# One order of VectorE's work in a local attention, and one layer of compressed blocks with its operands exchanged

## The reference, cut to what matters

```
def compress_blocks(kv, pe, w1, w2):
    B, G, S, dh = kv.shape
    ncmp = (S - CMP_LEN) // CMP_STRIDE + 1
    idx = (jnp.arange(ncmp) * CMP_STRIDE)[:, None] + jnp.arange(CMP_LEN)[None, :]
    blk = kv[:, :, idx] + pe
    flat = blk.reshape(B, G, ncmp, CMP_LEN * dh)
    return jax.nn.gelu(flat @ w1, approximate=False) @ w2
```

## Time and profile before

| | |
|---|---|
| median of 3 runs | 4155.18 us (4150.83 to 4158.11) |
| the profiled execution, its time | 4158.37 us |
| its span | 4157.0 us |
| busy: PE / DVE / ACT / POOL | 3893.0 / 2502.8 / 1586.3 / 870.8 us |
| mean granted clock of TensorE | 0.961 |
| local attention, first scores to output projection | 2564.84 to 2684.40 us |
| first `blocks` to first merge gate tile | 3708.92 to 3746.26 us |

### The profile page before, as it was taken

One profiled execution on the slowest core, in us unless ns is written; L12 is line 12 of the kernel. 1 busy time (PEld: TensorE's weight loads), 2 busy tenths in 40 slices (PEclk: granted clock), 3 DMA queues, 4 the chain that ended last, 5 costly groups with the idle time before them and its releaser, 6 DMA issues.

```text
span 4157.0 us, 58493 instructions
## 1 busy us (share of the span) xinstructions
PE 3893.0 (94%) x23644; PEld 3421.5 (82%) x23644; DVE 2502.8 (60%) x5047; ACT 1586.3 (38%) x2380; POOL 870.8 (21%) x404
## 2 busy tenths in 40 slices
PE   7998998899999999999999998898999999888799
PEld 4667888778888888778888876698999999888699
DVE  4554555379606884057766655585772677756575
ACT  2323444333234553221111124444565333347453
POOL 0002333034543333400000000068666000000000
PEclk9998999899999999999999998899999999988899
DMA  5231000123444556556767742056778678632254
GB/s 180 96 118 35 1 1 1 31 85 130 146 144 168 180 200 235 167 187 231 262 225 247 244 137 67 26 159 203 230 238 268 228 270 279 228 112 82 87 163 157
DMA packets 225500, 649.38 MB, mean 156 GB/s; under 512 B 20048, under 2 KB 89552, under 8 KB 217424
## 3 DMA queue, kind: packets, MB, share of 16 engines
q1 hardware_dynamic: 119296, 401.92, 30.5%
q10 hardware_dynamic: 105936, 243.73, 16.3%
HBM read 543.33 MB, written 101.71 MB: 155 GB/s over the span
## 4 chain that ended last, share of the span: by engine, by line
PE 85%; DVE 7%; ACT 4%; POOL 1%; ACTq 1%; DMA 1%; issue 1%; DVEq 0%
PE ps L133 84%; DVE g_b L80 2%; PE ps L136 1%; POOL lo L80 1%; ACTq L75 1%; DVE lo L80 1%; ACT hi L128 1%; ACT s_s L125 1%; DVE s_s L86 1%; ACT L124 0%; DVE s_st L98 0%; ACT n_s L125 0%; DVE n_rs L101 0%; DMA pcA<-pcga 0%; ACT g_b L124 0%
## 5 line engine op out<-in xcount | busy, mean ns | idle before, releaser
L128 ACT ACTIVATE hi<-ring 128x1024 fp32r<-128x1024 f32 x725 | 767.7, 1060 | 1037.6 <-PE ps L133 923.1
L80 POOL TENSOR_TENSOR lo<-ring,hi 128x1024 fp32r<-128x1024 f32 x288 | 722.5, 2512 | 1762.4 <-ACT hi L128 1762.2
L80 DVE TENSOR_TENSOR lo<-ring,hi 128x1024 fp32r<-128x1024 f32 x437 | 532.9, 1222 | 450.3 <-ACT hi L128 449.7
L133 PE MATMUL ps<-pahh,hi 128*128 128x512 f32 x1152 | 456.0, 396 | 17.8 <-POOL lo L80 10.8
L133 PE MATMUL ps<-pahh,lo 128*128 128x512 f32 x1152 | 450.5, 391 | 0.0
L133 PE MATMUL ps<-pahl,hi 128*128 128x512 f32 x1152 | 450.5, 391 | 0.0
L133 PE MATMUL ps<-pchh,hi 128*128 128x256 f32 x1152 | 336.5, 292 | 27.2 <-POOL lo L80 21.3
L133 PE MATMUL ps<-pchl,hi 128*128 128x256 f32 x1152 | 328.5, 285 | 0.0
L133 PE MATMUL ps<-pchh,lo 128*128 128x256 f32 x1152 | 328.4, 285 | 0.0
L133 PE MATMUL ps<-g_b,g_b 128*128 128x128 f32 x1984 | 259.8, 286 | 34.4 <-DVE g_b L80 25.4
L133 PEld LDWEIGHTS ps<-g_b,g_b 128*128 128x128 f32 x1984 | 243.0, 199 | 43.9 <-DVE g_b L80 29.5
(11 more groups left out here) (427 smaller groups left out, 9170.4 us busy)
## 6 DMA issues: line engine op xcount, KB each, us to landing
ring<-in_u SPq DMA_DIRECT2D x256, 512.0 KB, 3.7
ring<-in_v SPq DMA_DIRECT2D x256, 512.0 KB, 3.8
paA<-paga ACTq DMA_DIRECT2D x128, 256.0 KB, 2.3
paG<-paR ACTq DMA_DIRECT2D x16, 2048.0 KB, 8.5
paAg<-paA ACTq DMA_DIRECT2D x16, 2048.0 KB, 8.4
paGg<-paG ACTq DMA_DIRECT2D x16, 2048.0 KB, 16.9
late_w<-in_adat ACTq DMA_DIRECT2D x56, 512.0 KB, 3.7
ring<-in_ffn_up SPq DMA_DIRECT2D x44, 512.0 KB, 3.9
```

Source lines behind the costliest of these rows:

```text
L80: return Op(self.e.tensor_tensor(out, a, b, op) if self.real else None)
L128: return Op(self.e.activation(out, a, ACT.Copy, scale=scale) if self.real else None)
L133: return Op(self.e.matmul(out, l, r, start=start, stop=stop, skip_group_check=skip) if self.real else None)
```

## The change

The local attention's order of VectorE is woven with the newest unit first in each round; those of TensorE and ScalarE stay. In the compressed blocks, a piece of `blk` (30 columns) is now the stationary operand and 256 columns of the weights move: 16 matmuls in `blocks(q)` in place of 32, with the result [30 x 256], blocks on partitions. ScalarE's GELU is one instruction on [30 x 256] into a new tile `rows`; a new step `turn(q)` on TensorE transposes it in two pieces of 128 channels, VectorE copies the result into `hids[q]`, and `second(q)` waits for that copy. `turn(0)` stands behind `blocks(1)`, `turn(1)` behind `second(0)`, ahead of mo3. No DMA is added, removed or moved.

```diff
--- before.py
+++ after.py
@@ -142,14 +142,14 @@
         return self.mm(out, l[1], r[0], False, stop, skip=skip)
 
 
-def weave(gens, width):
+def weave(gens, width, newest=False):
 
     gens = list(gens)
     live = []
     while gens or live:
         if gens and len(live) < width:
             live.append(gens.pop(0))
-        for g in list(live):
+        for g in live[::-1] if newest else list(live):
             if next(g, False) is False:
                 live.remove(g)
 
@@ -1943,7 +1943,7 @@
                 act.cp(oT[0][rows, c, :], bank[6 + u % 2][rows, 0:256]).then_inc(s_exp, (u, "oh"))
 
             weave([attend_pe(u) for u in range(16)], W)
-            weave([attend_dve(u) for u in range(16)], W)
+            weave([attend_dve(u) for u in range(16)], W, newest=True)
             weave([attend_act(u) for u in range(16)], W)
             g0 = mods(1, 0, 0)[2]
 
@@ -2040,6 +2040,7 @@
         blk = [alloc(st, f"n_blk{q}", [128, 16, 2, 15]) for q in range(2)]
         w2 = [alloc(st, f"n_w2{q}", [128, 2, 64]) for q in range(2)]
         hids = [alloc(st, f"n_hid{q}", [128, 2, 30]) for q in range(2)]
+        rows = [alloc(st, f"n_hidr{q}", [30, 256]) for q in range(2)]
         gi, gf, e0, e1 = (alloc(st, f"m_{n}", [128, 2, 4]) for n in ("gi", "gf", "e0", "e1"))
         cs, ec = t["cs"], t["ec"]
         s_load = S("nsa_constants")
@@ -2074,14 +2075,19 @@
 
                 pe.wait_ge(s_blk, q)
                 pe.wait_ge(s_w1, q)
+                for m in range(16):
+                    op = pe.mm(bank[4 + 2 * q][0:30, 0:256], blk[q][:, m].rearrange("p g n -> p (g n)"),
+                               wk[q][:, m // 4, m % 4 * 256:m % 4 * 256 + 256], m == 0, m == 15)
+                op.then_inc(s_cmp, ("hidden", q))
+
+            def turn(q):
+                pe.wait_ge(s_hid, q)
                 for u in range(2):
-                    for m in range(16):
-                        op = pe.mm(bank[4 + 2 * q + u][:, 0:30], wk[q][:, m // 4, m % 4 * 256 + u * 128:m % 4 * 256 + (u + 1) * 128],
-                                   blk[q][:, m].rearrange("p g n -> p (g n)"), m == 0, m == 15)
-                op.then_inc(s_cmp, ("hidden", q))
+                    op = pe.tr(bank[5 + 2 * q][:, 30 * u:30 * u + 30], rows[q][:, 128 * u:128 * u + 128], ident[0:30, 0:30])
+                op.then_inc(s_cmp, ("turned", q))
 
             def second(q):
-                pe.wait_ge(s_hid, q)
+                pe.wait_ge(s_blk, ("turned", q))
                 pe.wait_ge(s_w2, 1)
                 b = bank[4 + 2 * q]
                 for gq in range(2):
@@ -2113,8 +2119,10 @@
                     pe.mm(b[:, 4:8], ones, gf[:, 0, :], True, False)
                     pe.mm(b[:, 4:8], bk("triF"), gf[:, 1, :], False, True).then_inc(s_cum, "cumulated")
                     blocks(1)
+                    turn(0)
                 elif n == 2:
                     second(0)
+                    turn(1)
                 else:
                     second(1)
 
@@ -2190,9 +2198,7 @@
 
             def hidden(q):
                 act.wait_ge(s_cmp, ("hidden", q))
-                for u in range(2):
-                    op = act.act(hids[q][:, u, :], bank[4 + 2 * q + u][:, 0:30], ACT.Gelu)
-                op.then_inc(s_hid, q)
+                act.act(rows[q][:, :], bank[4 + 2 * q][0:30, 0:256], ACT.Gelu).then_inc(s_hid, q)
 
             for n in range(4):
                 hi_to(mo[n])
@@ -2283,8 +2289,10 @@
             dve.cp(cs[:, :, :], bank[2][:, 0:8].rearrange("p (a b) -> p a b", b=4)).then_inc(s_mem, "cs")
             dve.wait_ge(s_mem, "cs")
             dve.tt(ec[:, :, :], gi[:, :, :], cs[:, :, :], SUB).then_inc(s_mem, "ec")
-            lo_to(mo[2])
-            lo_to(mo[3])
+            for q in range(2):
+                lo_to(mo[2 + q])
+                dve.wait_ge(s_cmp, ("turned", q))
+                dve.cp(hids[q][:, :, :], bank[5 + 2 * q][:, 0:60].rearrange("p (u n) -> p u n", u=2)).then_inc(s_blk, ("turned", q))
             dve.wait_ge(s_cmp, 0)
             dve.cp(t["kcm"][:, :], bank[4][:, 0:15])
             dve.wait_ge(s_cmp, 1)
```

## The result

| | before | changed |
|---|---|---|
| median (lowest to highest), 4 runs each | 4154.64 us (4150.83 to 4158.11) | 4119.55 us (4111.42 to 4122.75) |
| ratio, 95% interval | | 0.9913 (0.9896 to 0.9930) |
| profiled execution: span | 4157.0 us | 4119.8 us |
| local attention, first scores to output projection | 119.6 us | 87.8 us |
| first `blocks` to first merge gate tile | 37.3 us | 27.0 us |

What follows compares the result with a forecast made beforehand. It took the VectorE-ScalarE loop to bound the local attention and TensorE's clock the compressed blocks. Gains of 29.5 + 10.3 = 39.8 us off 4158.4 gave 4118.6, or 4115.4 us against the median; range 4107 to 4132.

Steps and rivals of the forecast that it cites:

- The loop of VectorE and ScalarE: Local attention: maximum, exponentials and second part alternate between the two engines with no matmul between; 6.81 us a round.
- Term 1: Local attention: VectorE's newest-first order cuts its loop with ScalarE, leaving TensorE as limit; gain 29.5 us, bounds 24 to 33.
- the rounds: Local attention, unit 4's to unit 15's scores: 11 rounds at 5.0 us, 55.0 in place of 72.5; gain 17.5 us.
- The tail: Local attention, end of unit 15's scores to output projection: 13 us with handoffs in place of 25.0; gain 12 us.
- the start: Local attention up to unit 4's scores: TensorE at half clock sets the pace in both orders; no gain.
- Term 2: Compressed blocks: exchanged operands keep the clock up, 27.05 us in place of 37.34; gain 10.3, bounds 2.7 loss to 12 gain.
- the stall: Compressed blocks: TensorE waits about 1.65 us ahead of `turn(1)` for the GELU behind mo2's sigmoid.
- the price of the old form: Compressed blocks with old operands: 37.34 us in the profile, limited by the clock; 6.85 us for 32 records at full clock.
- The clock held in the blocks: Rival claimed the opposite: with 30 of 128 columns used, `blocks` lose the full clock; 4128.4 us, chance 0.10.
- In the attention it held: Rival claimed the opposite: the clock fails for three attention rounds, 9.8 us in place of 5.0; 4130 us, chance 0.07.
- The slower case: Local attention: TensorE stays at half clock, 9.8 us a round for 16 units; 4182 us, chance 0.03.
- the order gains nothing: Local attention: VectorE's scores wait for TensorE instead, leaving only the exchange's gain; 4144.9 us, chance 0.03.

Runs made afterwards that it cites:

- e1: Kernel before with only VectorE's newest-first order in the local attention, old compressed blocks kept; 4124.89 us, ratio 0.9929 to the kernel before.
- e7: Changed kernel with VectorE's maximum over only the first 256 of 512 scores; profiled only, rounds 4.83 us each, attention 87.4 us.
- e4: Changed kernel with each compressed-block GELU put ahead of the sigmoid of the projection TensorE runs then; 4114.11 us, ratio 0.9907 to the kernel before.
- e10: Changed kernel with an early one-column exponential for the table load and the GELUs ahead of the sigmoids; 4113.80 us, ratio 0.9896 to the kernel before.

## Why the prediction was right, point by point

**What bounds the kernel.** Right for both stages. The loop of VectorE and ScalarE went with the order alone (e1), and the new limit is TensorE (e7).

**Term 1, 29.5 us.** The order alone measured 29.3 us in the time and 31.8 in its stage, so part of it does not reach the end or is lost in the scatter, and that 29.3 lies so close to 29.5 is in part luck. By the steps: the rounds took 4.83 us where I had taken 5.0, since I counted the scores at their 1.98 us of busy time; from start to start they are 1.91, and no handoff showed. That gave 19.4 in place of 17.5. The tail took 14.0 us, not 13: each of its rounds has a wait of 0.7 us of TensorE for ScalarE's copies. And the start was not quite equal: unit 4's scores began 18.8 us behind the first in place of 20.2, since TensorE's wait of 0.45 us for ScalarE ahead of the first output product was gone and the clock came back before the second transposes (1.09 us in place of 1.97).

**Term 2, 10.3 us.** This is the term that was mis-sized: 5.0 us in the time. The mechanism held. The 32 records took 0.216 us (0.22 forecast) at a grant of 1.00, mo1 and mo2 three us each, the stall 1.81 us (1.65 forecast). The first pair of profiles even shows 10.3 us, but by luck: it set the longest old stretch of three against the shortest new one of six. What failed is the price of the old form. I took it from one execution, in which the half clock lasted longest of the three that were profiled, and I held the new form to be free of it; in five of six profiles it had a piece of half clock behind the stall. The other weak step was to expect the gain to reach the end because no queue is moved behind: the hybrid attention there varies by 7 us with its clock, from 159.6 us at 0.90 to 166.5 at 0.84.

**The rivals.** The clock held in the blocks with 30 of 128 columns stationary, in eight profiles, so that rival is out (its price was also a little off: 3.0 us at the full clock and 4.0 us of work at half pace are 11.0, not 10.8). In the attention it held from unit 4 on; the transposes ran at 1.09 us for eight in all rounds from 2582.48 on, as the rows said. That goes against what the Trainium skill says of them (TensorE: Matmul & The Clock Gate, the paragraph on transpose mode), that the full clock does not engage; here the measurement decides. The slower case, TensorE at 9.8 us a round, showed only up to the second transposes, 2573.27 to 2582.48. That the order gains nothing is refuted by e1.

## What to carry to other kernels

Where an engine's queue alternates between producing for another engine and consuming its answer, put the newest item's producing step ahead of the older item's consuming step; then look which engine has the most work a round, since that is what is left, and read its work from start to start of its instructions. Compare two forms of a product by more than their pace at the full clock: here 30 moving columns were as quick as 256 (6.85 us by their records against 7.0), but the grant fell under them each time and the projection behind paid too (mo1 5.27 us in place of 3). A short wait that a change adds can cost more than itself in the same way: the stall of 1.8 us brought 1.5 us of half clock. A price that hangs on the clock should not come from one execution: profile the same kernel twice before it goes into a sum.

## What the runs showed of the hardware that I had not expected

- The same instructions took 32.7, 35.8 and 37.3 us with TensorE busy all the time, by the granted clock alone (mean 0.74, 0.67, 0.63).
- Stationary operands of 30 columns, with 256 columns moving, kept the grant at 1.00 through both `blocks` and the projection between, 17.6 us, in eight profiles of eight. 30 moving columns with 128 stationary lost it in each `blocks`, 2.4 to 5.2 us after its first matmul, in three profiles of three, and a mixture with full projections kept it for 12.3 us and lost it then.
- Behind an idle of 1.81 us of TensorE, which the trace shows in each of six profiles, the grant fell in five; without it (e4, e10) it stayed at 1.00.
- Stretches without any edit differ between executions: the start of the local attention lay between 2563.7 and 2569.0 us, and the hybrid attention took 159.6 to 166.5 us. A gain of 2 us, as that of e4, is seen in its stage and not in the time.
